# A conditioned mLSTM and short-convolution decoder step: later modulation fetches, one down tile ahead of the other, and the small products of a head in three groups

## The reference

```
for i in 0, 1:
    mod = (silu(c) @ ada_w[i] + ada_b[i])      # six vectors of 1024 per sequence
    hn  = rmsnorm(x) * g * (1 + mod[1]) + mod[0]
    out = mLSTM(hn)        if i == 0           # 8 heads, DK = 64, DV = 128
          short_conv(hn)   if i == 1
    x   = x + mod[2] * out
    hn  = rmsnorm(x) * g * (1 + mod[4]) + mod[3]
    f   = relu(hn @ w_up[i])^2 @ w_down[i]     # 1024 -> 4096 -> 1024
    x   = x + mod[5] * f
y = rmsnorm(x) * final_g
```

## Time and profile before

| what | value |
|---|---|
| median of 3 runs | 1326.35 us (1326.0 to 1326.61) |
| profiled execution, its own time | 1323.53 us |
| its span, first to last instruction | 1321.8 us |
| PE busy | 1277.1 us, 97% of the span |
| DVE, ACT, POOL busy | 771.2, 503.5, 366.5 us |
| granted TensorE clock, mean | 0.994 |
| main memory traffic | 169.34 MB, 128 GB/s on average |

### The profile page before, as it was taken

One profiled execution on the slowest core, in us unless ns is written; L12 is line 12 of the kernel. 1 busy time (PEld: TensorE's weight loads), 2 busy tenths in 40 slices (PEclk: granted clock), 3 DMA queues, 4 the chain that ended last, 5 costly groups with the idle time before them and its releaser, 6 DMA issues.

```text
span 1321.8 us, 26353 instructions
## 1 busy us (share of the span) xinstructions
PE 1277.1 (97%) x11305; PEld 1247.4 (94%) x11305; DVE 771.2 (58%) x1296; ACT 503.5 (38%) x792; POOL 366.5 (28%) x184
## 2 busy tenths in 40 slices
PE   5899999999999999999999999999999999999996
PEld 4799999999999999999999999999999999999996
DVE  2723435667757643643649818859858743824764
ACT  3532442222532451461453332213362551642721
POOL 2434434342300042032035344434310041050150
PEclk9999999999999999999999999999999999999998
DMA  9666214644456574474463132323232242342321
GB/s 331 212 192 162 79 55 120 224 151 142 122 182 193 162 221 128 145 237 130 133 190 96 51 110 80 96 83 86 60 96 80 66 129 63 96 129 64 96 65 68
DMA packets 242526, 169.34 MB, mean 128 GB/s; under 512 B 5851, under 2 KB 217055, under 8 KB 242282
## 3 DMA queue, kind: packets, MB, share of 16 engines
q1 hardware_dynamic: 215946, 121.33, 32.0%
q10 hardware_dynamic: 26304, 46.27, 10.7%
q0 software_dynamic: 160, 0.07, 0.0%
HBM read 160.70 MB, written 6.94 MB: 127 GB/s over the span
## 4 chain that ended last, share of the span: by engine, by line
PE 80%; DVE 9%; issue 3%; ACT 2%; DMA 2%; POOL 2%; ACTq 1%; SPq 0%; POOLq 0%; DVEq 0%
PE G L1921 40%; PE G L2041 17%; PE G L1947 9%; PE G L2077 5%; PE B L2105 3%; POOL wl L1086 2%; DVE acc L1272 1%; DVE hb L1395 1%; PE B L1907 1%; DVE small_s L1846 1%; DMA raw<-in_mlp_w_down 1%; ACT wh L586 1%; DVE yc L1845 1%; DMA xin<-in_x_sample 1%; DVE Xl L1409 1%
## 5 line engine op out<-in xcount | busy, mean ns | idle before, releaser
L1086 POOL TENSOR_TENSOR wl<-raw,wh 128x1024 fp32r<-128x1024 f32 x128 | 325.9, 2554 | 796.1 <-ACT wh L586 793.2
L586 ACT ACTIVATE wh<-raw 128x1024 fp32r<-128x1024 f32 x144 | 152.1, 1056 | 285.7 <-PE G L1921 127.7
L1921 PE MATMUL G<-Hh,wh 128*128 128x272 f32 x864 | 179.3, 289 | 0.0
L1921 PE MATMUL G<-Hh,wl 128*128 128x272 f32 x864 | 178.3, 288 | 0.0
L1921 PE MATMUL G<-Hl,wh 128*128 128x272 f32 x864 | 178.3, 288 | 0.0
L1921 PE MATMUL G<-Xh,wh 128*128 128x272 f32 x672 | 144.5, 296 | 1.0 <-POOL wl L1086 1.0
L1921 PE MATMUL G<-Xl,wh 128*128 128x272 f32 x672 | 138.8, 288 | 0.0
L1921 PE MATMUL G<-Xh,wl 128*128 128x272 f32 x672 | 138.3, 287 | 0.0
L1921 PEld LDWEIGHTS G<-Hh,wh 128*128 128x128 f32 x864 | 135.5, 188 | 1.0 <-issue 1.0
L1921 PEld LDWEIGHTS G<-Hl,wh 128*128 128x128 f32 x864 | 135.8, 189 | 0.0
L1921 PEld LDWEIGHTS G<-Hh,wl 128*128 128x128 f32 x864 | 135.1, 189 | 0.0
(11 more groups left out here) (385 smaller groups left out, 2729.9 us busy)
## 6 DMA issues: line engine op xcount, KB each, us to landing
raw<-in_mlp_w_up SPq DMA_DIRECT2D x64, 512.0 KB, 4.3
raw<-in_mlp_w_down SPq DMA_DIRECT2D x64, 512.0 KB, 4.2
aring<-in_ada_w ACTq DMA_DIRECT2D x60, 512.0 KB, 5.9
raw<-in_mlstm_w_in SPq DMA_DIRECT2D x24, 512.0 KB, 4.3
raw<-in_conv_w_in SPq DMA_DIRECT2D x24, 512.0 KB, 3.8
early<-in_ada_w SPq DMA_DIRECT2D x16, 512.0 KB, 12.0
free_l<-in_ada_w ACTq DMA_DIRECT2D x20, 256.0 KB, 9.0
raw<-in_mlstm_w_out SPq DMA_DIRECT2D x8, 512.0 KB, 4.9
```

The source lines that it names most:

```text
L586: nc.scalar.activation(wh[:, t % SLOTS], raw_of(t), ACT.Copy).then_inc(s_hi, 1)
L1086: nc.gpsimd.tensor_tensor(wl[:, t % SLOTS], raw_of(t), wh[:, t % SLOTS].bitcast(F32), ALU.subtract).then_inc(s_lo, 1)
L1921: last = mm(G[:, 2 * (g % 2) + hf, 0:HALF], w[:, s, k, :], x[:, k, hf * HALF:(hf + 1) * HALF], start=st, stop=en)
```

## The change

Three edits of order, and no instruction of any kind is added or removed.

1. *Modulation.* In `fast_up` on ACT, `quad_next` moves from behind the first `part_out` of pairs 0 and 2 to the end of the pair, behind the weight groups of the next. In the output projection the four `ada_pair`s no longer stand between tiles but ahead of the state products at four of their six places, and in the gate stage the first stands ahead of the sample numerators.
2. *Down tiles.* `fast_down` takes its steps from `lagging(4)` instead of `IN_STEP`: the first tile's k = 0 to 3, then the second's, then as before.
3. *Heads.* The scores of head m follow `head_product(m - 1)` directly, and `turn_head` moves from k = 0 to k = 2, so a tile has three groups.

```diff
-ADA_AFTER_W = {1: 0, 3: 1, 4: 2, 5: 3}
+ADA_AFTER_W = {2: 0, 3: 1, 4: 2, 5: 3}
+UPD_ADA = (0, 1, 3, 5)
...
                     part_out(u, p, 0)
-                    if ada is not None and p % 2 == 0:
-                        quad_next(ada, p // 2)
...
                         elif i:
                             hi(u + KT + i)
+                    if ada is not None and p % 2 == 0:
+                        quad_next(ada, p // 2)
...
-                for pos, o in IN_STEP:
+                for pos, o in lagging(4):
...
+            def scores(h):
+                a, pr = h // 2, slice(DK * (h % 2), DK * (h % 2) + DK)
+                for i in range(NJ):
+                    c = slice(i * P, (i + 1) * P)
+                    last = mm(B5[:, c], kT[pr, a, c], qT[pr, a, c], start=True, stop=True)
+                last.then_inc(s_s, 1)
...
-                    if k == 0 and h >= 2:
-                        turn_head(h - 2)
-                    if k == 1:
-                        if h:
-                            pe.wait_ge(s_pr, h)
-                        else:
-                            pe.wait_ge(s_sp, 1)
...
+                    if k == 1 and h == 0:
+                        pe.wait_ge(s_sp, 1)
+                        scores(0)
                     if k == 2:
+                        if h >= 2:
+                            turn_head(h - 2)
...
                 if m:
                     head_product(m - 1)
+                    scores(m)
...
+            def numerators():
+                ada_pair(4 * 3)
+                sample_numerators()
+
-            O_STEPS = {(1, 0): lambda: turn_head(H - 2), (1, 5): lambda: turn_head(H - 1), (3, 1): sample_numerators, (6, 2): sample_turned}
+            O_STEPS = {(1, 0): lambda: turn_head(H - 2), (3, 1): numerators, (6, 2): sample_turned}
...
                     sample_scores()
+                    turn_head(H - 1)
...
-                if m in ADA_AFTER_O:
+                if m in ADA_AFTER_O and ADA_AFTER_O[m]:
...
                     g = UPD_AT.index((m, k))
+                    if g in UPD_ADA:
+                        ada_pair(4 * 4 + UPD_ADA.index(g))
...
-            mixed(T_WOUT, G_WOUT, 4, Yh, Yl, x_ready(X_Y), between=state_products, ada_after=ADA_AFTER_W)
+            mixed(T_WOUT, G_WOUT, 4, Yh, Yl, x_ready(X_Y), between=state_products, ada_after={})
```

## The result

| | us |
|---|---|
| before, median of 4 | 1326.17 (1323.77 to 1326.61) |
| after, median of 4 | 1310.17 (1309.41 to 1310.94) |
| ratio | 0.9876, interval 0.9862 to 0.9889 |
| span of the profiled executions | 1321.8 before, 1307.7 after |

The change is faster by 16.0 us, or 1.2%. The forecast was 10.6 us and 1315.7, with a range that ended at 1312.0: the direction is right, and the gain was half as large again as forecast.

A forecast was written before the change was run, and what follows sets the result against it. PE, busy 97% of the span, was taken as the bound. Savings of 6.3 + 2.45 + 0.8 + 1.0 = 10.6 us gave 1312.9 for the profiled execution and, scaled, a median of 1315.7, range 1312.0 to 1320.5.

The forecast's parts named there:

- Term 1: First layer's fast up units: six PE waits for ACT's copies, held up by modulation fetches, go: 6.3 us.
- the stall moves: Fast up units: long fetch issue at the new place delays the next weight group; 1322, or 1319 with half back; chance 0.12.
- the pieces land too late: PE's modulation groups after pairs 1 and 3 wait for late fetches: slower, 1334 at 16.5 us landings; chance 0.03.
- Term 2: Second layer's fast down units: three PE waits for POOL's low weights at the second tile go: 2.45 us.
- Term 3: Fewer separate groups of small products: 0.8 us for seven heads in value tiles, 1.0 us for five modulation pairs.
- the groups are worth nothing: Joints between small-product groups cost what breaks did, so only the stall and down-tile gains remain: 1317.6; chance 0.13.
- Term 3's modulation pairs: Five modulation pairs joining other groups each save a run's break: 0.2 us each, 1.0 in all, from 0 to 1.6.
- 0.8 us to spare: Output projection, second modulation pair: 7.0 us between fetch and use, against landings of 5.7 plus 0.5 for the second issue.
- From the profile to the median: Last step of the sum: 1312.9 for the profiled execution; the same share, 0.80%, off the median gives 1315.7.

The follow-up runs named there:

- experiment 6: The changed kernel with the scores of head m ahead of the head product instead of behind it: 1315.0 us, ratio 0.9916.
- experiments 3 and 4: The kernel before with only the down tiles' order changed, 1323.97 us; and with only the scores moved behind the head product, transposes left, 1321.25 us.
- the second group: Later runs on another chip: the changed kernel again, unaltered, 1311.95 us, ratio 0.9896 to the kernel before, with three variants of it beside.
- experiment 7: The changed kernel with the scores dealt out one for one among the state products of the head product: 1308.54 us, ratio 0.9871.

## Why the prediction missed

**The reading of the bound was right.** PE was the bound, and each wait that it named has gone.

**Term 1, right, a little low:** 6.85 us where 6.3 was the number. The stalls, the room for 2.4 to 3.0 us of issue (2.83 in the first one) and the arrival in time all came out as said. The six stalls lost 6.4 by the distance of starts. The other 0.45 lies behind them: the second product after each stall starts 0.20 us behind the first instead of 0.126 (438.32 to 438.53 in the first), 0.075 apiece. Landings of `free_l` took 5.9 to 10.7 us there and those of the 512 KB pieces up to 9.6, and PE waited for none. The rivals "the stall moves" and "the pieces land too late" didn't come.

**Term 2, right, a little low:** 2.7 for 2.45, three times 0.90. The distance of starts was 1.08, and 0.25 of it is pace, which leaves 0.83. The other 0.07 apiece are again the late second product behind the wait: the two rows at 1075.91 last 0.49 us together instead of 0.41.

**Term 3 is where it failed.** Its sentence was "two unlike groups may lose 0.08 to 0.1 at each joint. I take 0.12 per head for 7 heads, 0.8 us, between 0 ... and 2.0." What the breaks are worth came out nearly as written, 0.14 a tile in experiment 6. But the bound of 2.0 allowed only for breaks, and left out that two neighbours can overlap: 0.60 us a tile by experiment 6, 4.2 us over seven tiles (by the rows 0.54, from 1.95 to 1.41). 0.60 + 0.14 over seven tiles are 5.2 us, where term 3 had 0.8 for the heads. The column "64*128" with the halves in the code pointed at it, and the trace before had small products that overlap. The state update of the earlier trace rows is one row of it:

```profile
275.21 1.54 PE L2373 MATMUL B<-vtok_s,kam 32*64 32x129 f32 x24
```

Its 24 products took 1.47 us, 0.061 each, where eight products of nearly the same length took 1.09 alone, 0.136 each; the code puts them in turn into the two halves of the array's columns. Two halves of the rows stood side by side only in the sample scores (16 products of 32 columns, at 212.69): there the first product of the other half starts 6 ns behind the last one ahead of it (212.838, 212.844 in the records). The rival "the groups are worth nothing" asked the same wrong question.

**Term 3's modulation pairs:** 0.8 us was counted for four joins in the output projection, and the stage lost 0.25. Two waits took 0.5 each, the one for the piece, for which I had found "0.8 us to spare", and the one for `XP`, which I didn't foresee. Without them the joins give 0.7, as said within 0.1. The room of 0.8 was counted from a fetch issued when the first pair is done. It was issued 1.1 us later, behind ACT's copy. This is a new wait for a piece in PE's list, which the prediction had named as a sign of being wrong.

**From the profile to the median:** I scaled by the share, 1323.53 to 1326.35, which assumes that profiled and other runs lose the same. The stalls that the change removes vary among executions (6.4 us before, 7.6 and 8.1 in experiments 3 and 4), and the profile of before had them short. The edit that removes them brought 8.3 us by medians and 6.2 in its trace. That is a likely cause of the 1.9 us by which the miss, 5.4, is larger than in the traces, 3.5; it is argued and not shown, and the second group, with a gain of 13.8, doesn't have these 1.9 us at all. The medians of the three single edits add to 6.2 + 8.3 + 2.3 = 16.8, so the edits don't help or hinder each other by more than can be measured.

## What to carry to other kernels

Before you price a small product by its own duration, read which rows of the array it uses, "64*128" in a row of the profile, and which partitions its operands start in: two kinds with 64 rows in opposite halves, next to each other in the program, cost as much as the longer kind alone if they are written in turn (1.09 us for 14 products that took 1.95 apart), and one product over all 128 rows between them undoes it. When an edit removes a stall whose length hangs on what else is being issued, take its cost from several executions, not from one. Look at what comes *after* a stall as well: 0.075 us behind each one here, and 1.5 us of half clock behind one.

## What of the hardware was unexpected

- Two fp32 products of 64 rows in opposite halves start 3 to 7 ns apart in the records of experiment 7, and a pair takes 0.11 us. The first pair of a run took 0.20 (135.12 to 135.32).
- Program order need not alternate for it. With six rows of state products followed by eight of scores, the first score started at 135.13, ahead of the fourth state product at 135.24 in the records, and 0.54 of the possible 0.86 us of overlap came by itself; written in turn, all of it.
- A stall of 2.48 us on PE (from start to start) was followed by 3.4 us at half the clock, which cost 1.5 us more. One of 2.35 us in another kernel, and the six of 0.87 to 1.43 us before, were followed by the full clock.
- Behind each of the nine waits of the kernel before, the second product starts 0.20 us behind the first instead of 0.126, so a wait costs 0.075 us more than its own length.
- Five fetches hold ACT's queue for 2.83 us at one place and 3.55 at another (1.42 + 2.13), and nothing on ACT but the instruction in front of them runs meanwhile.
